# Moving the early feed-forward loads and GpSimd's row sums in the sample tile of a hybrid decoder step

## The reference, cut to what matters

```python
hn = rmsnorm(x, norm1_g)
proj = hn @ w_in                              # 1024 -> 3608
o_a, h_a = gla_chunked(q, k, v, log_a, st_gla)          # 4 heads, state 64 x 128 per head
o_b, h_b = gdn_chunked(qd, kd, vd, g, beta, st_gdn)     # 4 heads, state 128 x 128 per head
mix = concat(rmsnorm(o_a) * silu(gate_a), rmsnorm(o_b) * silu(z_b))
x = x + mix @ w_out                           # the residual rows
hn2 = rmsnorm(x, norm2_g)
up, ffn_new = causal_dwconv(hn2 @ w_up, st_ffn, ffn_conv_w)
x = x + (silu(a_f) * b_f) @ w_down
y = rmsnorm(x, norm_f_g)
```

## Time and profile before

| | |
|---|---|
| three runs | 3204.51, 3210.66, 3211.82 us; median 3210.66 us |
| the profiled execution | 3208.88 us, span of its records 3207.2 us |
| mean granted TensorE clock | 0.987 of full speed |
| PE busy | 3118.8 us, 97% of the span |
| DVE, ACT, POOL busy | 62%, 26%, 14% of the span |
| the sample tile's DMA queue | one hardware queue, issued by SP |

### The profile page before, as it was taken

One profiled execution on the slowest core, in us unless ns is written; L12 is line 12 of the kernel. 1 busy time (PEld: TensorE's weight loads), 2 busy tenths in 40 slices (PEclk: granted clock), 3 DMA queues, 4 the chain that ended last, 5 costly groups with the idle time before them and its releaser, 6 DMA issues.

```text
span 3207.2 us, 51997 instructions
## 1 busy us (share of the span) xinstructions
PE 3118.8 (97%) x20269; PEld 2023.9 (63%) x20269; DVE 1996.0 (62%) x4791; ACT 834.3 (26%) x1743; POOL 448.4 (14%) x823
## 2 busy tenths in 40 slices
PE   7999999999999999997899999999999999999998
PEld 4555555555555555544677777777766677777665
DVE  2556666565555666656466666656776666666668
ACT  2222333322322333334221221121132122222113
POOL 1000000000000000002431111111153211111110
PEclk9999999999999999997899999999999999999999
DMA  7022222222222222227511111111133111111102
GB/s 246 28 68 86 87 86 67 86 87 68 72 70 70 87 86 85 63 74 210 163 50 43 40 40 53 40 40 40 52 127 120 42 51 40 40 40 40 53 27 79
DMA packets 223169, 236.08 MB, mean 74 GB/s; under 512 B 14204, under 2 KB 167332, under 8 KB 222931
## 3 DMA queue, kind: packets, MB, share of 16 engines
q1 hardware_dynamic: 222931, 232.81, 23.3%
HBM read 203.10 MB, written 29.67 MB: 73 GB/s over the span
## 4 chain that ended last, share of the span: by engine, by line
PE 51%; DVE 0%; issue 0%; ACT 0%; DVEq 0%
PE mlp_bank L2206 34%; PE mlp_bank L2280 15%; PE mlp_bank L2294 2%; PE mlp_bank L2286 0%; DVE arena L2619 0%; DVE acc L2716 0%; ACT raw L2398 0%; DVE arena L2620 0%; PE mlp_bank L2305 0%; PE mlp_bank L2292 0%; DVE arena L2627 0%; DVE arena L2624 0%; DVE raw L2587 0%; DVE y_parts L2688 0%; DVE raw L2593 0%
## 5 line engine op out<-in xcount | busy, mean ns | idle before, releaser
L723 PE MATMUL mixer_bank<-arena,hnt 128*128 128x451 f32 x2048 | 866.3, 554 | 9.3 <-DMA arena<-in_w_in_dram 8.5
L2206 PE MATMUL mlp_bank<-arena,ws 128*128 128x256 f32 (+1 forms) x2816 | 646.1, 383 | 2.7 <-DVE raw L2593 2.7
L2206 PEld LDWEIGHTS mlp_bank<-arena,ws 128*128 128x128 f32 x2816 | 534.9, 190 | 85.6 <-DVE raw L2593 3.5
L723 PEld LDWEIGHTS mixer_bank<-arena,hnt 128*128 128x128 f32 x2048 | 365.1, 190 | 302.6 <-issue 294.0
L2280 PE MATMUL mlp_bank<-arena 128*128 128x512 f32 x1120 | 493.8, 592 | 1.0 <-DVE arena L2627 1.0
L2688 DVE TENSOR_TENSOR acc<-acc,mlp_bank 128x512 f32<-128x512 f32 x560 | 370.8, 686 | 55.4 <-PE mlp_bank L2280 54.7
L2280 PEld LDWEIGHTS mlp_bank<-arena 128*128 128x128 f32 x1120 | 212.7, 190 | 235.6 <-issue 205.6
L2655 DVE SCALAR_TENSOR_TENSOR mcv<-raw,cf,mcv 128x512 f32<-128x512 f32 (+2 forms) x352 | 263.1, 763 | 50.7 <-ACT mcv L2369 41.9
L2206 PE MATMUL mlp_bank<-arena 128*128 128x256 f32 (+1 forms) x1056 | 249.4, 386 | 5.6 <-PEq L2798 4.6
L757 PE MATMUL mixer_bank<-wo,th 128*128 128x512 f32 x512 | 248.3, 609 | 4.1 <-DMA wo<-in_w_out_dram 3.5
L2206 PE MATMUL mlp_bank<-arena,wu 128*128 128x256 f32 (+1 forms) x1056 | 246.0, 383 | 0.9 <-ACT raw L2398 0.9
(11 more groups left out here) (385 smaller groups left out, 3382.8 us busy)
## 6 DMA issues: line engine op xcount, KB each, us to landing
wo<-in_w_out_dram SPq DMA_DIRECT2D x260, 256.0 KB, 2.8
arena<-in_w_up_dram SPq DMA_DIRECT2D x44, 512.0 KB, 5.0
wu<-in_w_up_dram SPq DMA_DIRECT2D x44, 512.0 KB, 5.0
arena<-in_w_down_dram SPq DMA_DIRECT2D x40, 512.0 KB, 4.2
arena<-in_w_in_dram SPq DMA_DIRECT2D x7, 1804.0 KB, 16.7
xc<-in_x_t_dram SPq DMA_DIRECT2D x16, 512.0 KB, 4.1
xt<-in_x_prompt_dram SPq DMA_DIRECT2D x16, 512.0 KB, 5.0
xr<-in_x_prompt_dram SPq DMA_DIRECT2D x16, 512.0 KB, 3.7
```

Source lines behind the costliest of these rows:

```text
L723: x = pe.matmul(bank[ring(g)][0:N, 0:GW], hnt[:, k, 0:N], w[:, k, g * GW:(g + 1) * GW], start=(k == 0), stop=(k == KT - 1))
L2206: x = pe.matmul(out[:, 0:N], left[:, k, :], xb[:, slot, k, g * N:(g + 1) * N], start=first and k == 0, stop=k == HK - 1, skip_group_check= ...
```

## The change

On SP, the first half of `early_x` and the early weights move behind the last prompt tile's `w_out` chunks, and the second half of `early_x` moves behind the sample's `w_out` chunks, ahead of `out_stores`. On GpSimd, the four differences move behind `mixer`, ahead of the scalings. Nothing is computed differently, and no DMA or operation is added or removed.

```diff
             sp.wait_ge(s_hs_stored, 16 * (TILES // 2 + 1))
-            for g in range(2):
+
+            def early_x(g):
                 for half, part, slot in X_PARTS:
...
-            for e in range(2):
-                sp.dma_start(wu0[:, e, :, :], w_up.rearrange("(k p) n -> p k n", p=C)[:, :, e * DFF:e * DFF + C])\
-                    .then_inc(s_early_w, 16)
-            sp.dma_start(cwt, ffn_taps).then_inc(s_early_w, 16)
+            def early_w():
+                for e in range(2):
+                    sp.dma_start(wu0[:, e, :, :], w_up.rearrange("(k p) n -> p k n", p=C)[:, :, e * DFF:e * DFF + C])\
+                        .then_inc(s_early_w, 16)
+                sp.dma_start(cwt, ffn_taps).then_inc(s_early_w, 16)
...
             last_wo(8, 16)
+            early_x(0)
+            early_w()
...
                 sample_wo(i, wo_s[i - 4], s_wos_loaded)
+            early_x(1)
             out_stores(t, slice((t - 1) * C, t * C), slice((t - 1) * C, t * C), C,
...
             gp.memset(mq_gla[:, :, :, :], 0.0).then_inc(s_hs_cleared, 1)
+            mixer(TILES, TILES + 1, True, True)
             def difference(out, a, b):
...
             difference(b[T4], b[B21], b[T2]).then_inc(s_early_made, 1)
-            mixer(TILES, TILES + 1, True, True)
             gp.wait_ge(s_og_done, TILES + 1)
```

## The result

| | median | runs | ratio to before, 95% interval |
|---|---|---|---|
| before | 3208.36 us | 14 | |
| after | 3217.78 us | 14 | 1.0031 [1.0023, 1.0038] |

The change makes the kernel slower by 9.4 us, 0.3% of its time. The profiled execution of after took 3217.62 us, its span is 3215.9 us, its mean granted clock 0.986.

What follows compares the result with a forecast made beforehand. The sample tile's end is bound by VectorE's wait at L1498 for the queued residual store. 0 at the front, +8.7 at the store, 0 on GpSimd: 3208.88 + 8.7 = 3217.6 us, 80% range 3211 to 3224.

Steps and rivals of the forecast that it cites:

- The mechanism: At L1498, VectorE waits for the residual store, which lands behind everything issued ahead of it in the DMA queue: 8.7 us later.
- The queue's term: Ahead of L1498: 2.4 us to landing, 17.3 for early loads, 12.0 for sixteen chunks, 1.3 for the store; landing at 1537.6.
- The start of the early loads: On SP, chunk 15 and the early loads behind it are issued at 1504.6 instead of 1508.9.
- chunk 8: At the front, issued at about 1496.3 behind the prompt states' stores, landing at 1498.9, with TensorE there at 1497.0.
- chunks 10 and 11 behind them at full clock: At the front, TensorE's pieces behind the transposes run at full clock, part of putting chunk 15 at 1504.6.
- The front's gain: TensorE's chunk waits shrink; 3 us earlier readiness at L1498, hidden by the store wait, so 0 in the sum.
- The stretch behind L1498: From L1498 to the first feed-forward matmul, TensorE idle then at the low clock as before: 25.1 us kept.
- GpSimd at nothing: Moved differences and later scalings cost 0 on GpSimd, with 9.7 us of cover only because the store is late.
- The other signs: L1530 wait gone, chunk waits at most 2 us, store at about 1538 with some 15 us wait, no GpSimd wait at L1885.
- A: Rival at the residual store: late by its issue alone, not queued behind loads, landing at 1532; +3, 3212; chance 0.18.
- B: Rival on GpSimd: differences twice as long, 23.3 us, first scaling late for VectorE; +10.6, 3219.5; chance 0.08.
- C: Rival at the front: its 3.1 us come through because the store lands at 1525.8 or before; 3205.8; chance 0.06.

Runs made afterwards that it cites:

- e1: After, with the residual store of the last prompt tile issued ahead of the second four row loads instead of behind them; 3215.02 us.
- e7: After, with the residual store issued between the sample's chunks 10 and 11; 3211.16 us.
- e8: After, with three further loads of 512 KB that nothing needs ahead of the residual store; 3221.15 us.
- e11: After once more, unchanged, as a second profiled execution; 3215.51 us (one run).
- e9: After, with the stores of the prompt's states issued ahead of chunk 4 instead of between chunks 7 and 8; 3215.17 us.
- e3: Before, with only the second four row loads moved behind the sample's chunks, ahead of the residual store; 3213.07 us.
- e10: e6 with GpSimd's order of after, the differences behind its small operations and ahead of the scalings; 3207.62 us.
- e4: After, with all eleven early loads issued behind the residual store, GpSimd's order as in after; 3225.49 us.
- e6: Before, with states' stores ahead of chunk 4, residual store between chunks 10 and 11, weights behind the `xr` reload, second rows behind the normalised rows' store; 3203.49 us.
- e2: Before, with only GpSimd's four differences moved behind `mixer`, ahead of the scalings; DMA order as before; 3210.96 us.

## Why the prediction was right

Forecast were 3217.6 us and slower; the median is 3217.78. Taken from the reload, the prediction's landing is 1537.6 - 1460.0 = 77.6 us and its stretch 25.1; the two executions of after have 80.2 and 77.6, 21.9 and 22.1. The forecast was counted from the profiled execution of before, 3208.88 us; counted from the median that was known then, 3210.66, it would have been 3219.4.

**The mechanism: right.** The store lands in its place in the queue. e1, e7 and e8 move it by its place or by what stands ahead, and the time follows: less by 3.5 and 5.9 us, more by 4.1.

**The queue's term: right in size.** From the first early load to the landing 33.0 us were forecast (2.4 + 17.3 + 12.0 + 1.3); measured were 33.2 (1541.03 - 1507.87), 32.4 in e11 and 33.9 in e9. As a sum, the middle between the rates of the earlier trace rows held. Its parts are less even: the first seven loads took 15.1 us for 13.3 (2.4 + 10.9), the chunks 11.4 for 12.0, the last four row loads with the store 6.7 for 7.7. The slices above show 179 to 220 GB/s where the first loads start, and up to 414 later. The limit of about 358 GB/s per core that the page "DMA: Bandwidth & Descriptors" of the Trainium skill states (section Bandwidth) is no ceiling in this trace either. The same section calls it the share of a core when both cores of a memory domain stream; this kernel runs on one core.

**The start of the early loads: too early by 0.7 to 2.4 us.** Forecast was 44.6 us after the reload (1504.6), measured 47.0 and 45.2. Two steps of the front came later than I had them. The first is chunk 8, which I had landing at 1498.9. Counted from the reload, TensorE takes it up 1.1 us later in after (1500.88 - 0.84 = 1500.0) and 1.2 in e11. The wait for it was nearly in my numbers, 1.9 us (1498.9 - 1497.0) for the 2.2 measured; TensorE and the chunk both came later. The second is "chunks 10 and 11 behind them at full clock". In after the clock granted from 1502 to 1504 us was 0.61, and the first piece behind the wait took 2.88 us; in e11 it stayed at 1.00 and the same piece took 1.98. The clock makes the 1.8 us between the two executions.

**The front's gain: right.** The gate ahead of L1503 starts 62.1 us after the reload (1522.97), 64.5 before (1524.52): 2.4 us were won where I took 3, and they are swallowed by the store, as forecast.

**The stretch behind L1498: wrong.** "TensorE's stretch behind L1498 is in the same state as before ... so I keep its 25.1 us" failed by 3.2 us, and by 3.0 in e11. A stretch that is not 25 us long was one of the prediction's own signs of being wrong. Two things differ. The larger is the clock. In both executions of after the second half of the sample projection was granted the high clock, 1.9 us for it in place of 3.6, and the products ahead of it (L1066) took 1.1 us in place of 1.9: 2.5 us together in the first of them. The other is a step of VectorE, before and after:

```profile
1531.39 1.26 DVE L1904 SCALAR_TENSOR_TENSOR o_ss<-qss,o_ss 32x4 f32<-32x4 f32 x1
```

```profile
1543.53 0.15 DVE L1909 SCALAR_TENSOR_TENSOR o_ss<-qss,o_ss 32x4 f32<-32x4 f32 x1
```

Before, it meets GpSimd's second scaling, the gate behind it (L1770) is late, and TensorE waits 0.86 us for that gate. In after the store is so late that the scaling has ended, and TensorE does not wait: 0.9 us less. What follows is 0.2 us longer. So the scalings do cost VectorE something; the prediction looked only at whether they themselves had grown.

The errors of landing and stretch have opposite signs. In the first execution they nearly cancel (80.2 + 21.9 = 102.1 against 77.6 + 25.1 = 102.7); in e11 the landing is right and the sum is 3.0 us too high (99.7). So 0.2 us between forecast and median is luck; 2 to 3 us would be the honest accuracy of this sum. Why the clock came back sooner stays open: it did so in after twice and in e8, behind waits of 14.5 to 20.2 us at L1498, and not in e9 behind one of 15.6 us, nor in e1, e3 and e7 behind 6.4 to 10.7. The window of e9 that answers to the last one shown of after:

```profile
1548.00:1550.00 2.00, 2.00 (x24) 0.79 (x16) 0.00 (x0) 0.00 (x0) 0.00 (x0) 0.51 0.00 0
```

The engine is as busy as in after, at half the clock.

**GpSimd at nothing: right here, and for the reason given.** The first rows land 9.9 us after the early loads begin, not 8.8, so the differences run from 1517.8 to 1529.6 in place of 1513 to 1525. The store is later too, and 9.0 us of cover are left (1542.32 - 1533.36) for the 9.7 forecast. The cover is the late store's: e7 uses it up and waits 0.2 us, e10 shows the price without it. What the prediction did not have is the form of the price. It looked for slower differences; the differences kept their 11.65 us nearly (11.85 and 12.49), and in the first execution VectorE's steps beside them grew.

**The other signs.** VectorE's wait at L1530 is gone but for 0.3 us (L1535 now). TensorE's wait for a chunk is 2.2 us, a little over the 2 that were allowed. The store lands at 1541.0 for 1538, with a wait of 16.6 us for some 15, and the addition behind L1503 waits for nothing from GpSimd.

**The rivals.** A falls: the store took 8.8 us from issue to landing, not 2.4 to 2.9. B falls for this change, since the scalings ended before L1503; e4 shows that the same wait costs 19.4 us where the rows come late. C falls: nothing of the front came through. What it named does exist, though: e6 lets the front through by taking the store out of the way, and gains 4.1 us on before.

## What to carry to other kernels

When loads are moved out of one wait's way in a single queue, list what now stands behind them, stores above all: a store that guards the reuse of a buffer is on the path as much as a load. Count the bytes between its new and its old place and divide by the rate that the busy windows show; that gave the queue's part of this delay within 1 us. And a cost that is hidden by the delay which the same change makes is not free: it shows when that delay is mended.

## What was not expected of the hardware

A VectorE step of almost no work can be held up by GpSimd. From the view of the line in e10, over the whole run (duration of one in ns, min/median/max):

```profile
L1736 DVE TENSOR_TENSOR begcol<-egcol,nbeta x17: 161/163/3201, 108.4 to 1510.6; 128x4 f32<-128x4 f32 x16, 32x4 f32<-32x4 f32 x1
```

Sixteen of the seventeen take 0.16 us, the one that meets the start of the differences 3.20. It starts at 1510.56 and ends at 1513.76. The fourth of GpSimd's sixteen operations ends at 1513.75:

```profile
1513.03 0.72 POOL L687 TENSOR_TENSOR arena<-arena 128x256 f32<-128x256 f32 x1
```

These four operations are the first of the four differences. GpSimd works them off without a gap, then waits for a semaphore, and the fifth starts at 1513.82. So the step looks stopped, not slowed, until GpSimd first pauses. In e2 another step met them, L1790, and took 3.14; it ends at 1516.88, the fourth operation at 1516.73. The four masks in the midst of the differences grew from 1.41 to 3.0 to 3.4 in after, e2, e7, e8, e9 and e10. In e1, and in e11, which is after once more, the masks kept 1.41 us and the differences took 12.59 and 12.49; there one operation of GpSimd takes 2.0 to 2.1 us beside the masks. One of the two engines gives way, and which it is changes from execution to execution of one kernel.

The step of the stretch behind L1498 (L1904, 32x4 elements) shows the same with single instructions. In after, e3, e8, e9 and e11 GpSimd's scalings have ended before it, and it takes 0.15 us. In the other nine executions it meets the second scaling and takes 0.54 to 1.84 us, and in all nine it ends 0.01 to 0.02 us after one of the four operations of that scaling does. The operation it meets in the kernel before ends at 1532.64, the step at 1532.65:

```profile
1530.73 1.91 POOL L698 TENSOR_TENSOR arena<-arena,egrow 128x1024 f32<-128x1024 f32 x1
```

The page "SBUF — State Buffer" of the Trainium skill (section SBUF: two separate sides) says that VectorE, with two SBUF inputs, and GpSimd share a pair of ports by an exclusive lock, held for a whole instruction, and that the other one stops. That an operation on 32x4 stops agrees with it, and L1904 agrees to the end of one instruction. The length of the stop at the differences does not follow from it: one difference operation takes 11.89 / 16 = 0.74 us, and the step was held for four of them.
